# A decoder trunk step on one core: gate projections by seven block products per tile pair

## What is computed

```python
h = rms(x) * (1 + scale) + shift              # modulated by c @ w_ada
z = h @ w_in                                  # 2048 -> 13456: q k v qi ki wi ga u gb ma mb
idx = top_k(indexer(qi, wi, ki), k)           # 128 keys a prompt query, 256 a sample query
attn = gathered_attention(q, k, v, idx)       # samples: over a paged cache
pool = mixed_window_means(u)                  # windows 2, 4, 8, 16
a  = (attn * silu(ga)) @ w_a_proj             # 2048 x 2048
bb = (pool * silu(gb)) @ w_b_proj             # 1024 x 2048
m  = sigmoid(ma) * a + sigmoid(mb) * bb       # ma, mb: 2048 columns each of z
y  = rms_final(x + gate * (m @ w_out))
```

## Time and profile before

| | us |
|---|---|
| three runs | 2070.01, 2070.62, 2073.64 (median 2070.62) |
| profiled execution | 2073.4 |
| its span | 2069.9 |
| TensorE busy | 1997.7 (97%) |
| DVE, POOL, ScalarE busy | 1140.1, 860.8, 494.5 |
| moved by DMA | 258.70 MB, 125 GB/s in the mean |

### The profile page before, as it was taken

How to read it: one execution, slowest core, us unless ns; L and a number is a source line. 1 busy time by engine, 2 the same in 40 slices (tenths; PEclk the granted TensorE clock), 3 DMA queues, 4 the chain that set the end, 5 groups by cost and what they waited for, 6 DMA issues and landing times.

```text
span 2069.9 us, 35770 instructions
## 1 busy us (share of the span) xinstructions
PE 1997.7 (97%) x15122; PEld 1813.3 (88%) x15138; DVE 1140.1 (55%) x1510; ACT 494.5 (24%) x620; POOL 860.8 (42%) x700
## 2 busy tenths in 40 slices
PE   4789999999999999999999999999999999999997
PEld 1379999897999999999999999999999998887775
DVE  2346666566777777775566566667644621142223
ACT  3222222343222222222111222221222411132222
POOL 0044444554343434333444344444566433344441
PEclk7789999999999999999999999999999999999999
DMA  9953223443323232333333233334476565534323
GB/s 340 362 166 84 69 74 81 141 145 110 105 71 91 69 88 77 85 91 109 84 83 82 73 91 91 91 91 112 133 212 197 173 202 164 176 107 150 102 101 123
DMA packets 325028, 258.70 MB, mean 125 GB/s; under 512 B 6555, under 2 KB 275031, under 8 KB 323623
## 3 DMA queue, kind: packets, MB, share of 16 engines
q1 hardware_dynamic: 312911, 228.10, 37.5%
q0 software_dynamic: 5120, 16.77, 2.5%
q10 hardware_dynamic: 6912, 12.59, 1.8%
HBM read 246.42 MB, written 11.48 MB: 125 GB/s over the span
## 4 chain that ended last, share of the span: by engine, by line
PE 87%; DMA 5%; DVE 3%; issue 1%; ACT 1%; POOL 1%; SPq 0%; POOLq 0%; DVEq 0%; ACTq 0%
PE acc L1373 68%; PE ps L1762 8%; DMA ring<-in_w_ada 4%; PE ps L1569 2%; PE ps L1559 2%; PE ps L1443 1%; POOL wlo L466 1%; PE ps L1549 1%; DVE big L1215 1%; ACT whi L567 1%; PE ps L1700 1%; PE ps L1481 1%; PE acc L1753 1%; PE ps L1618 1%; PE acc L1387 1%
## 5 line engine op out<-in xcount | busy, mean ns | idle before, releaser
L466 POOL TENSOR_TENSOR wlo<-raw,whi 128x512 fp32r<-128x512 f32 (+1 forms) x616 | 787.1, 1309 | 1009.5 <-ACT whi L567 1009.5
L1373 PE MATMUL acc<-act_hi,whi 128*128 128x260 f32 x3904 | 810.5, 289 | 5.3 <-POOL wlo L466 3.4
L1373 PE MATMUL acc<-act_hi,wlo 128*128 128x260 f32 x3904 | 786.5, 283 | 0.0
L1373 PE MATMUL acc<-act_lo,whi 128*128 128x260 f32 x3904 | 784.9, 283 | 0.0
L1373 PEld LDWEIGHTS acc<-act_hi,whi 128*128 128x128 f32 x3904 | 604.1, 189 | 42.6 <-issue 37.0
L1373 PEld LDWEIGHTS acc<-act_hi,wlo 128*128 128x128 f32 x3904 | 601.7, 189 | 0.0
L1373 PEld LDWEIGHTS acc<-act_lo,whi 128*128 128x128 f32 x3904 | 601.5, 188 | 0.0
L567 ACT CAST whi<-raw 128x2048 fp32r<-128x2048 f32 (+1 forms) x154 | 280.8, 1823 | 1052.6 <-PE acc L1373 891.0
L1762 PE MATMUL ps<-whi,act_hi 128*128 128x512 f32 x256 | 103.1, 403 | 0.0
L1762 PE MATMUL ps<-whi,act_lo 128*128 128x512 f32 x256 | 101.1, 395 | 0.0
L1762 PE MATMUL ps<-wlo,act_hi 128*128 128x512 f32 x256 | 101.1, 395 | 0.0
(11 more groups left out here) (273 smaller groups left out, 2075.6 us busy)
## 6 DMA issues: line engine op xcount, KB each, us to landing
raw<-in_w_in SPq DMA_DIRECT2D x106, 1024.0 KB, 5.7
ring<-in_w_ada SPq DMA_DIRECT2D x32, 1024.0 KB, 14.2
raw<-in_w_a_proj SPq DMA_DIRECT2D x16, 1024.0 KB, 6.9
gate_unit<-in_w_ada SPq DMA_DIRECT2D x16, 1024.0 KB, 5.4
raw<-in_w_out SPq DMA_DIRECT2D x16, 1024.0 KB, 5.1
raw<-in_w_b_proj SPq DMA_DIRECT2D x16, 512.0 KB, 4.6
x_tok<-in_x_prompt SPq DMA_DIRECT2D x4, 1024.0 KB, 17.0
att_dram<-silu_ga ACTq DMA_DIRECT2D x16, 256.0 KB, 3.7
```

What stands on the lines that cost most here:

```text
L466: return nc.gpsimd.tensor_tensor(wlo[p][:, a:b], raw[p][:, a:b], whi[p][:, a:b].bitcast(F32), ALU.subtract)
L1373: last = mm(acc[p][:, a, 0:HALF], w, x[:, k, a * HALF:(a + 1) * HALF], start=(k == 0 and n == 0), stop=(k == kt - 1 and n == 2))
```

## The change

**Seven products.** The mb and ma gates, 32 tiles, are computed as 16 pairs of tiles. The depth of 2048, the pair's 256 output columns and the 520 tokens are each cut in two, so a pair is a 2 x 2 by 2 x 2 product of blocks: four weight blocks A11, A12, A21, A22 (1024 x 128) and four token blocks (1024 x 260). Instead of eight block products, seven are made, of plain blocks (named 1, 2, 4) and of sums (3, 5, 6, 7: Winograd's form), and their results are added up. A block product is 8 slices x 3 matmuls of 260 columns, 24 matmuls into one bank (`block`). The order in a pair is 1 5 6 3 4 7 2; in the first pair it is 1 5 6 3 7 2 4. The operands have four slots, the halves of `whi` and `wlo`: `SLOT = (0, 1, 2, 3, 0, 1, 3)`.

- The token sums (three blocks) are made once by POOL in stage D, between the low parts of its tiles (`token_sums`, `token_low`); a fourth one (`last_hi`, `last_lo`), half by POOL and half by DVE, when `act_hi` has been read for the last time by stage D.
- For each pair DVE makes four weight sums of 1024 columns (`s1` to `s4`), the low parts of two blocks (`sum_low`), and seven additions of 260 columns to take the results out (`quarter`). POOL makes the low parts of the other five blocks, each as two halves of 512 (`pair_low`). ScalarE casts seven times 1024 columns (`pair_high`), copies two banks (`snap`) and takes the exponential of the pair before (`gate_exps`, 1040 columns). SP loads a pair's blocks of 512 KB one by one as their places come free (`load_block`).
- The samples' attention is spread over the pairs: sample b's transposes lie in pair b + 6, the rest of it in pair b + 7 (pairs are counted from 0).

**Gates through DRAM.** exp(-z) of each pair is stored in `one_dram` (`keep_gates`). ma comes back as two loads of 2.1 MB into `big2` ahead of w_a; mb comes back tile by tile during w_b, into `mb_back`, where ScalarE adds 1 (`mb_one`) and DVE takes the reciprocal. The gated pool output goes to DRAM as well and is split after it has come back.

**w_b behind w_a.** Stage X, 16 tiles of w_b, now runs after W, the 16 tiles of w_a. m is split there: `m_high` on ScalarE, `m_low` on POOL.

**Top-k rounds.** 24 of the 32 rounds are in the heads (one and a half a head, with parts behind the softmax's maxima and behind prob), the other 8 in stage D: `D_ROUNDS = (1, 2, 1, 2, 1, 1, 0, 0)`, each behind a gate product of D.

The core of the diff:

```diff
+SLOT = (0, 1, 2, 3, 0, 1, 3)
+FIRST_ORDER, ORDER = "1563724", "1563472"
+FIRST_BANKS, BANKS = (0, 1, 0, 1, 2, 3, 1), (0, 1, 2, 3, 0, 1, 2)
+ON_POOL = (0, 1, 4, 5, 6)
+D_ROUNDS = (1, 2, 1, 2, 1, 1, 0, 0)
...
@@ SP @@
+        for g in range(PAIRS):
+            if g:
+                keep_gates(g - 1)
+            if g + 1 < PAIRS:
+                sp.wait_ge(*since("sum_ready", 4 * g + 4))
+                if g:
+                    sp.wait_ge(*since("pair_lo", 5 * g + 3))
+                    load_block(g + 1, A22)
+                load_block(g + 1, A21)
+                load_block(g + 1, A11)
...
+                sp.wait_ge(*since("pair_lo", 5 * g + 5))
+                load_block(g + 1, A12 if g else A22)
...
@@ POOL @@
+        def pair_low(g, i):
+            product = product_at(g, i)
+            pool.wait_ge(*since("pair_hi", 7 * g + i + 1))
...
+            minus(slot_lo(i)[:, 0:512], source[:, 0:512], slot_hi(i)[:, 0:512].bitcast(F32))
+            minus(slot_lo(i)[:, 512:1024], source[:, 512:1024], slot_hi(i)[:, 512:1024].bitcast(F32)
+                  ).then_inc(S("pair_lo"), 1)
...
+        for g in range(PAIRS):
+            for i in ON_POOL:
+                pair_low(g, i)
+                if g == 0 and i == 1:
+                    last_block_sums()
+                if g == 0 and i == 5:
+                    last_block_low()
+                if i == 4:
+                    sample_rows(g - 1)
...
@@ ScalarE @@
+        for g in range(PAIRS):
+            n, c = g - 1, cbuf[g % 2]
+            if g:
+                pair_high(g, 3)
+            sample_exp(n)
+            if g:
+                gate_exps(g - 1)
...
+            snap(g, 0, c[:, 0, LEFT])
+            pair_high(g, 4)
...
+            snap(g, 1, pbuf[:])
+            pair_high(g, 5)
...
+            pair_high(g, 6)
+            sample_keys(n)
...
+                pair_high(g + 1, 0)
+                pair_high(g + 1, 1)
+                pair_high(g + 1, 2)
...
+        for j in range(2, KT):
+            hi(Q_X + j // 2, j % 2, n=1024)
+            m_high(j - 2)
+            act.dma_start(mb_back[j % 2][:], one_dram[j]).then_inc(counts(f"mb_landed{j % 2}"), 16)
+            if j >= 4:
+                mb_one(j - 1)
...
@@ DVE, pairs after the first @@
+            s4(g)
+            if g > 1:
+                after_pair(g - 1)
+            sample_att(n - 1)
+            sample_max(n)
+            sum_low(g, 2)
+            sample_norm(n)
+            sum_low(g, 3)
+            s3(g)
+            sample_pages(n)
+            sample_pst(n)
+            after_sixth(g, c)
+            after_third(g, c)
+            sample_out(n)
+            if g + 1 < PAIRS:
+                s1(g + 1)
+                s2(g + 1)
+            after_fourth(g, c)
+            after_seventh(g, c)
...
+        for j in range(KT):
+            i, p = j // 2, j % 2
+            dve.wait_ge(*since("mb_one", j + 1))
+            step(v.reciprocal(mb_back[p][:], mb_back[p][:]))
...
+            dve.wait_ge(unit_done[p], Q_X + i + 1)
+            v.tensor_tensor(halves(mb_back[p][:]), accv[p], halves(mb_back[p][:]), ALU.mult).then_inc(acc_free[p], 1)
+            dve.wait_ge(acc_free[p], N_X + i + 1)
+            v.tensor_tensor(big2[:, j, :], mb_back[p][:], big2[:, j, :], ALU.add).then_inc(S("m_ready"), 1)
```

More of the change, by code:

```diff
@@ L392, in _, with keep_gates @@
[L392 to L398, removed]
-        sp.wait_ge(S("sa_oT"), NB)
[L400 to L403, removed]
+        def keep_gates(g):
+            sp.wait_ge(*since("rows_exp", g + 1))
+            sp.dma_start(one_dram[2 * g:2 * g + 2].rearrange("t p n -> p t n"), cbuf[g % 2][:]
+                         ).then_inc(counts(f"gate_kept{g % 2}"), 16)
@@ new lines, in _ @@
+        sp.wait_ge(*since("sum_ready", 4 * PAIRS))
+        sp.wait_ge(*since("pair_lo", 5 * PAIRS - 2))
+        load(Q_W, 0, cols(w_a, 0), first=True)
+        sp.wait_ge(S("sa_oT"), NB)
+        for n in range(STAGES):
+            load_att(n)
+        sp.wait_ge(*since("pair_lo", 5 * PAIRS))
+        load(Q_W, 1, cols(w_a, P), first=True)
+        sp.wait_ge(*since("prod_done", 7 * PAIRS - 1))
+        for p in range(2):
+            sp.wait_ge(*since(f"gate_kept{p}", 16 * 6))
+        sp.dma_start(big2[:, 0:8, :], one_dram[KT:KT + 8].rearrange("t p n -> p t n")).then_inc(counts("ma_landed0"), 16)
@@ L417, in _ @@
         for n in range(2, 2 * 8):
[L418 removed]
+            load(Q_W + n // 2, n % 2, cols(w_a, P * n))
             if n == 4:
@@ L435, in _ @@
         sp.dma_start(gate_dram[:, 512 * 3:512 * 4], gate_row[:]).then_inc(S("gate_stored"), 16)
+        for j in range(2, KT):
+            load(Q_X + j // 2, j % 2, cols(w_b, P * j))
+        for kq in range(2):
+            load(Q_G, kq, quarter(w_out, kq, 0))
         for kq in range(2, 4):
@@ new lines, in _ @@
+        for n in range(1, 9):
+            att_high(n)
+        gate_exps(PAIRS - 1)
+        hi(Q_W, 1, first=True)
+        for n in range(9, KT):
+            att_high(n)
+        for j in range(8):
+            hi(Q_W + 1 + j // 2, j % 2)
+        act.wait_ge(*since("pool_back", 16))
+        for j in range(8):
+            if j < 6:
+                hi(Q_W + 5 + j // 2, j % 2)
+            nc.scalar.copy(pool_hi[:, j, :], pool_raw[:, j, :]).then_inc(counts("pool_hi_ready"), 1)
+        for j in range(2):
+            hi(Q_X, j, n=1024)
@@ new lines, in block @@
+        def block(g, i):
+            product = product_at(g, i)
+            x_hi, x_lo = TOKENS[product]
+            if i in ON_POOL:
+                pe.wait_ge(*since("pair_lo", 5 * g + ON_POOL.index(i) + 1))
+            else:
+                pe.wait_ge(*since("sum_low", 2 * g + i - 1))
+            for k in range(8):
+                wh, wl = slot_hi(i)[:, k * P:(k + 1) * P], slot_lo(i)[:, k * P:(k + 1) * P]
+                for n, (w, x) in enumerate(((wh, x_hi), (wh, x_lo), (wl, x_hi))):
+                    last = mm(bank_of(g, product), w, x[:, k, :], start=(k == 0 and n == 0), stop=(k == 7 and n == 2))
+            last.then_inc(counts("prod_done"), 1)
@@ L1693, in gate_product @@
+        first_pair()
+        for g in range(1, PAIRS):
+            pair(g)
         def gate_product(u):
```

676 lines of the change are left out of this document (498 added, 178 removed), and 3 rows, old and new, of the table COUNTS_ON.

## The result

The changed kernel takes **2114.6 us** (median of four runs, 2110.6 to 2120.4) against 2071.4 for the kernel before: ratio **1.021** (95% interval 1.018 to 1.024). Slower was right; 2084 us was 31 us too low, and the range to 2112 did not hold it.

A forecast was written before the change was run, and what follows sets the result against it. TensorE, busy for 97% of the span, was taken to bound the kernel; -46.1 - 1.7 + 27 + 11 + 4 + 0 + 6 + 13 = +13 us gave 2084 us on the median, range 2048 to 2112.

The forecast's parts named there:

- What the change gives (-46.1, -1.7): Gate stages: 384 fewer matmuls of 0.120 us save 46.1 us; one TensorE wait for POOL ahead of ma goes, 1.7.
- Without the sample's work the loop is 17.6 to 22.4 us, +0.8 in seven: Seven pairs without sample attention: queue loop through block A12 against TensorE's 20.2 us, so +0.8 us each.
- 512 KB land in 4.6 us: Pairs: landing time assumed for a weight block's load within the queue loop.
- Sample pairs 25.8: Eight pairs with sample attention: loop of 23.5 to 28.3 us, middle 25.8, against TensorE's 23.1; +2.7 each.
- The signs named for the forecast being right: Sample pairs near 26 us, TensorE waiting for POOL, DVE's 1024-column operations over 1.6, w_b tiles 6.6, first pair 31.
- The two engines take turns, an instruction each: DVE and POOL sharing SBUF: they alternate by instruction, and a meeting costs each side about 1.2 us.
- First pair +11: First pair: DVE and POOL sums meet from the last pooling tile's end, delaying block 5 and last operand; +11 us.
- Pooling stage +4: Pooling stage: top-k rounds behind gate products delay two window chains, and POOL's token sums add meetings; +4 us (0 to 12).
- Heads 0: Heads: eight more top-k rounds fit where DVE was idle, cost 0; up to 2.3 us in each of 15 otherwise.
- Into w_a +6 (1 to 12): Entry to w_a: ScalarE's casts wait for the last pair's block 5 and stages loaded behind 2.1 MB of gates; +6 us.
- w_b +13: w_b stage: a loop of DVE's steps and ScalarE's casts and +1 takes 6.6 us a tile; +13 us (9 to 23).
- The clock, 0.03 and +6: First pair: rival that waits of 6 us lower TensorE's clock, two blocks slower, +6 us, 2090 us; chance 0.03.

The follow-up runs named there:

- e3: Changed kernel with SP issuing the next pair's blocks A21 and A11 ahead of A22, which waits for POOL's third low part: 2100.9 us, ratio 1.013.
- e5: Changed kernel with every block load of the pairs cut to its first half, 256 KB for 512 (gates wrong): ratio 1.012.
- c10: c1 plus DVE making A12's low part (from second pair), first pair's block 5 cast early, new rows issued behind next pair's casts: 2065.9 us, ratio 0.9963.
- e7: Changed kernel with block loads halved and, from the third pair, DVE's block sums and low parts replaced by fills (gates wrong): ratio 1.0026.
- e8: Changed kernel with POOL's gathers moved between its low parts of blocks 6 and 7, instead of ahead of both: ratio 1.0208.
- e1: Changed kernel with ScalarE copying banks 0 and 1 out before it waits for the last pooling tile, in the first pair: 2113.7 us, ratio 1.020.
- c5: c1 plus gathers between low parts 6 and 7, first new rows split over two pairs, block 5's cast ahead of the pooling store: ratio 1.0020.
- e4: Changed kernel with ScalarE's +1 of gate j-1 ahead of casting m(j-2), and the output stage's first casts ahead of the last +1: 2103.6 us, ratio 1.015.
- c1: Changed kernel with e1, e3, e4 and, at w_a, second-half attention loads ahead of gates, third and fourth weight tiles ahead of later reloads: 2077.9 us, ratio 1.0025.

## Why the prediction was wrong

- **What the change gives (-46.1, -1.7)** stands: a block's 24 matmuls into one bank take 2.88 us at full clock (168 in 20.15 in the last pair), and that pair runs without a wait.
- **"Without the sample's work the loop is 17.6 to 22.4 us, +0.8 in seven": this step failed.** The second to seventh pair took 24.7 us each, 22 us more than forecast together, 6 of them clock. The loop that I priced goes through A12; the one that set the pace goes through A21 and A11, which SP issues behind A22's wait for POOL. e3 shows its order (12 us in the pairs), e5 its bytes (14 us there), c10 the burst in the fourth pair. The meetings stand in the same loop: with both cut in e7 the pairs take 371.3 us.
- **The term mis-sized in it: "512 KB land in 4.6 us".** They took 7.4 to 13.7 where it counted. I took the median of loads that nobody waited for, from a stage where one is issued every 17 us; here three follow each other, in sample pairs beside 1 MB of gathers and up to 1 MB of new rows, and the last of the three counts.
- **Sample pairs 25.8**: about right in size, 25.2 over the eight, but by another loop and with 2 us of clock in one of them: luck, not the mechanism. The signs named for the forecast being right nearly all came true (DVE's 1024-column operations took 1.73 us on average, TensorE waited 27.0 us for POOL's low parts), and none of them looked at a landing.
- **"The two engines take turns, an instruction each"**: too simple. Where one meets one it holds. Where DVE meets POOL's four in a row, it waited 4.5 us, and beside six in a row 6.5 (e8). By the Trainium skill (SBUF — State Buffer, SBUF: two separate sides) whoever starts first has the shared ports for the whole instruction; the trace agrees on that for single meetings, and shows a loser that loses several times in a row.
- **First pair +11**: 13 measured, with 2.9 of clock; the place was wrong. TensorE stood from its third block, not its fifth, because ScalarE's copy stands behind the pooling store (10.0 us). e1 and c5 show the rest as forecast: the pair ends 33 us after its start whatever waits come before.
- **Pooling stage +4**: 2.2. **Heads 0**: 0.
- **Into w_a +6 (1 to 12)**: 19.3. The splits behind the gates were seen, but taken too small (8.9 us of waits for them); not seen was SP's queue: each tile's weights come behind all reloads issued before (4.5 us of wait) and 5.9 us of clock behind the three waits. The forecast said that the DRAM traffic costs nothing unless a reload is waited for; it was other loads that waited for the reloads.
- **w_b +13**: 9.4 and nothing net in the output stage; 6.3 us a tile for 6.6. The mechanism was right, and e4 shows it.
- **The clock, 0.03 and +6**: it is 19.4 us. I treated it as a rival beside the others, in one place, though every rival with long waits had to pay it. Eight such places, charged with 1.5 to 3 us each, would have put the forecast at some 2096 to 2108 (an estimate from the losses above), though it had foreseen only a few of these waits. By the rule of the Trainium skill (TensorE: Matmul & The Clock Gate, HAM oscillation) which I cited and weighed at 0.03, idle gaps between bursts throttle the array again; the trace agrees in eight places. One of the waits of 2.3 us (at 1394) had no fall behind it.

Open: why the third load lands 3 us behind the first even with no gathers or new rows beside it, and how much of the longer landings is the gathers and how much the new rows, was not separated. Nor was the first pair's last-operand chain taken apart.

## What to carry to other kernels

When a change leaves the bounding engine one operation of slack instead of many, price the loads by their worst landing beside everything that is issued in the same microseconds, and walk through the DMA queue's order as through an engine's: here a few lines of it were worth 12 to 17 us, and a few others 13. Charge every new wait of several microseconds of TensorE twice, once for itself and once for the slower matmuls behind it, before comparing with what removed matmuls give. A saving of 46 us of matmuls was worth 8 in the best version found.

## What was not expected of the hardware

- A VectorE operation with both inputs in SBUF waited out four GpSimd operations in a row (5.75 us for 1.23, in c1), which were not slowed at all (5.01 us for four), and in e8 six (7.71 us).
- The granted clock fell behind waits as short as 2.1 us (e1, at 1223), at a price of 1.4 to 3 us each, but not behind each of that length: 2.34 us in the changed kernel (at 1394), 2.50 in c10 (at 1347) and 2.93 in e3 (at 1216) had no fall.
- A load of 256 KB took 10.08 us to land beside the burst of new rows, where the median of its kernel is 3.3 (e7's chain and page):

```profile
1252.13 10.08 DMA raw<-in_w_in
```
```profile
raw<-in_w_in SPq DMA_DIRECT2D x64, 256.0 KB, 3.3
```
